# Gathered token rows turned on VectorE in 32x32 blocks instead of on TensorE, in one layer of a hybrid trunk with experts

## The reference

```python
def swiglu(x, w_gate, w_up, w_down):
    return (jax.nn.silu(x @ w_gate) * (x @ w_up)) @ w_down
...
def moe_ffn(xf, w_router, router_bias, w_eg, w_eu, w_ed, w_sg, w_su, w_sd):
    ...                                  # scores, groups, top 8 of 64, weights top_w
    x_pad = jnp.concatenate([xf, jnp.zeros((1, D), xf.dtype)], axis=0)
    def expert_block(args):
        tok, e = args
        xb = x_pad[tok]
        return swiglu(xb, w_eg[e], w_eu[e], w_ed[e])
    y = lax.map(expert_block, (buf_tok.reshape(n_blocks, MOE_BLK), block_e)).reshape(P, D)
    y = y * buf_w[:, None].astype(y.dtype)
    routed = jnp.zeros((N + 1, D), y.dtype).at[buf_tok].add(y)[:N]
    return routed + swiglu(xf, w_sg, w_su, w_sd)
```

## Time and profile before

| | |
|---|---|
| median of 3 runs | 1494.25 us (1493.85 to 1494.46) |
| span of the profiled execution | 1490.5 us |
| median less that span | 3.75 us |
| TensorE busy | 1470.0 us, 99% |
| VectorE busy | 660.9 us, 44% |
| ScalarE busy | 299.4 us, 20% |
| GpSimd busy | 663.8 us, 45% |
| front, up to the first routed matmul | 526 us |

### The profile page before, as it was taken

The page is one execution under the profiler, slowest core; times in us unless marked ns, Lnnn a source line. Parts: engine busy times, 40 slices in busy tenths (PEclk is TensorE's granted clock), DMA queues, the critical chain, the costliest instruction groups (busy, mean ns, idle before and its releaser), DMA issues.

```text
span 1490.5 us, 24090 instructions
## 1 busy us (share of the span) xinstructions
PE 1470.0 (99%) x6687; PEld 652.1 (44%) x6688; DVE 660.9 (44%) x892; ACT 299.4 (20%) x568; POOL 663.8 (45%) x626
## 2 busy tenths in 40 slices
PE   7999999999999999999999999999999999999998
PEld 3556556556565433333333333333333333333333
DVE  2344444454355454444444444444444444444432
ACT  1223323323323201111111111111111111111110
POOL 3010222212302525566655666655666556665541
PEclk9999999999999999999999999999999999999999
DMA  9511201202155579999998988888899898998938
GB/s 346 192 56 37 78 29 50 79 8 71 52 219 202 177 280 283 304 292 295 300 356 253 320 285 259 256 254 252 262 351 348 275 321 265 300 300 250 329 58 213
DMA packets 74637, 330.06 MB, mean 221 GB/s; under 512 B 14647, under 2 KB 16184, under 8 KB 48932
## 3 DMA queue, kind: packets, MB, share of 16 engines
q1 hardware_dynamic: 45140, 249.62, 45.1%
q0 software_dynamic: 29456, 79.93, 22.7%
HBM read 282.74 MB, written 65.11 MB: 233 GB/s over the span
## 4 chain that ended last, share of the span: by engine, by line
PE 94%; DMA 3%; DVE 1%; issue 1%; ACT 0%; SPq 0%; DVEq 0%; POOL 0%; POOLq 0%; ACTq 0%
PE psP L733 55%; PE psW L733 30%; PE psT L892 5%; DMA area<-x_dram 1%; DMA wts<-in_w_in_dram 1%; PE psW L955 1%; PE psW L784 1%; PE psT L826 0%; PE psT L810 0%; PE psT L741 0%; DMA out_dram<-area,sidx 0%; PE psW L761 0%; DMA x_dram<-area,sidx 0%; DVE area L1423 0%; DVE st_s L1433 0%
## 5 line engine op out<-in xcount | busy, mean ns | idle before, releaser
L733 PE MATMUL psP<-wts,bias 128*64 (+1 forms) x1296 | 574.0, 595 | 1.2 <-issue 1.1
L733 PE MATMUL psP<-area,bias 128*64 128x512 f32 x1264 | 559.4, 595 | 0.0
L733 PE MATMUL psW<-wts,area 128*64 (+2 forms) x1592 | 426.2, 592 | 0.7 <-ACT area L1305 0.5
L733 PEld LDWEIGHTS psP<-wts,bias 128*64 128x64 f32 (+1 forms) x1296 | 172.4, 138 | 336.4 <-issue 336.4
L689 POOL DMA_INDIRECT out_dram<-area,sidx x79 | 173.0, 2190 | 286.9 <-ACT area L1250 215.5
L733 PE MATMUL psP<-wts,area 128*128 128x512 f32 (+1 forms) x704 | 287.8, 560 | 6.2 <-DMA wts<-in_w_in_dram 4.8
L733 PEld LDWEIGHTS psW<-wts,area 128*64 128x64 f32 (+1 forms) x1592 | 150.1, 147 | 249.3 <-issue 247.7
L689 POOL DMA_INDIRECT x_dram<-area,sidx x79 | 247.0, 3127 | 26.6 <-issue 24.0
L1656 DVE COPY wts<-wts 128x2048 f32 x79 | 97.0, 1228 | 298.6 <-issue 298.6
L1648 DVE COPY area<-wts 128x4096 f32 x79 | 181.5, 2297 | 25.2 <-issue 20.7
L733 PEld LDWEIGHTS psP<-wts,area 128*128 128x128 f32 x704 | 131.1, 191 | 136.3 <-issue 126.5
(11 more groups left out here) (224 smaller groups left out, 870.3 us busy)
## 6 DMA issues: line engine op xcount, KB each, us to landing
wts<-in_w_exp_gate_dram SPq DMA_DIRECT2D x64, 1024.0 KB, 8.9
wts<-in_w_exp_up_dram SPq DMA_DIRECT2D x64, 1024.0 KB, 12.2
wts<-in_w_exp_down_dram SPq DMA_DIRECT2D x64, 1024.0 KB, 7.0
wts<-in_w_in_dram SPq DMA_DIRECT2D x4, 2048.0 KB, 18.0
area<-in_x_dram SPq DMA_DIRECT2D x8, 512.0 KB, 4.1
wts<-in_w_out_dram SPq DMA_DIRECT2D x1, 4096.0 KB, 18.4
area<-u_dram SPq DMA_DIRECT2D x16, 256.0 KB, 2.9
xn_dram<-area POOLq DMA_DIRECT2D x8, 512.0 KB, 3.0
```

The source lines that it names most:

```text
L733: return nc.tensor.matmul(out_, lhsT, rhs, start=start, stop=stop)
```

## The change

TensorE's `t_job` and VectorE's `read_xT` go. A new VectorE function `turn_x` reads the gathered rows from SBUF and writes `xT[par]` by sixteen transposing operations. One operation takes 32 tokens (a quarter of the partitions of `xg`) and, of each of the eight 128-column blocks, 32 columns; it turns eight 32x32 blocks and writes them to a quarter of the partitions of `xT[par]`. All bytes end where they were before. `turn_x` waits for the gather itself; the gathers wait for `s_xT_ready` instead of `s_xg_t`, with the same counts. In the loop `turn_x` stands where `read_xT` stood; in the written-out start `copy_dn(0)` and `copy_dn(1)` now stand ahead of the turn. Both weight copies stay on VectorE.

```diff
--- before.py
+++ after.py
@@ -53,6 +53,7 @@
     FT = FE // P
     assert NT == 8 and KT == 8 and NKV == 2 and DC == DA == 512 and FT == 2
     HB = P // 2
+    QUAD = 32
     JMAX = S * TOPK // P + NE // 2
     JT = JMAX + 6
     MIN_JOBS = S * TOPK // P
@@ -277,7 +278,6 @@
         s_tab_t = sem("tab_t")
         s_tab = sem("tab")
         s_sc_tab = sem("sc_tab")
-        s_xg_t = sem("xg_t")
         s_gu = sem("gu")
         s_silu = sem("silu")
         s_h_ready = sem("h_ready")
@@ -659,7 +659,7 @@
 
             def gather(j, par, copies):
 
-                pool.wait_ge(s_xg_t, j - (NSH + 1))
+                pool.wait_ge(s_xT_ready, j - (NSH + 1))
                 nc.gpsimd.tensor_copy(gidx[:, par:par + 1], tab_i[:, bass.ds(j - NSH, 1)]).then_inc(s_idx_cp, 1)
                 pool.wait_ge(s_idx_cp, copies + 1)
                 carry(pool)
@@ -669,7 +669,7 @@
 
             def first_gather(r):
                 if r >= 2:
-                    pool.wait_ge(s_xg_t, r - 1)
+                    pool.wait_ge(s_xT_ready, r - 1)
                 pool.indirect_dma_start(out=xg[:, r % 2], out_offset=None, in_=xn_dram[:, :],
                                         in_offset=bass.IndirectOffsetOnAxis(ap=tab_i[:, r:r + 1], axis=0),
                                         bounds_check=S - 1, oob_is_err=False).then_inc(g_ld[r % 2], 16)
@@ -883,15 +883,6 @@
                     t_x(NN)
                 out_project(T, 1)
 
-            def t_job(j, par, nth):
-
-                pe.wait_ge(g_ld[par], nth * 16)
-                if not (isinstance(j, int) and j == NSH):
-                    pe.wait_ge(s_xT_ready, j - NSH)
-                for k in range(KT):
-                    i = nc.tensor.transpose(psT[:, k, :], xg[:, par, k * P:(k + 1) * P], ident[:, :])
-                i.then_inc(s_xg_t, 1)
-
             def gate_up_late(t, ks):
                 buf, ld = shared_place(NSH + t)
                 if 0 in ks:
@@ -1053,8 +1044,6 @@
             down(2)
             t_h(4, psP[:, side(4), :])
             down(3)
-            t_job(NSH, 0, 1)
-            t_job(NSH + 1, 1, 1)
 
             def jobs(i, ks):
                 for k in ks:
@@ -1063,7 +1052,6 @@
                     now = pe.value_load(ring_i[0:1, bass.ds(r + 1, 1)], min_val=1, max_val=NE)
                     gate_up_halves(r + NSH, k, (now % NSLOT) * SLOTW)
                     down_halves(r + NSH - 1, (was % NSLOT) * SLOTW)
-                    t_job(r + NSH + 2, k, i + 2)
                     t_h(r + NSH, psW[:, 0, :])
 
             one = routed_jobs(pe, 1, jobs, counts)
@@ -1607,10 +1595,15 @@
             conv_gate(tiles[0])
             y_conv_rms(tiles[0])
 
-            def read_xT(j, par):
-                dve.wait_ge(s_xg_t, j - (NSH - 1))
+            def turn_x(j, par, nth):
+                dve.wait_ge(g_ld[par], nth * 16)
                 dve.wait_ge(s_gu, j - 1)
-                V.tensor_copy(xT[par], psT[:, :, :]).then_inc(s_xT_ready, 1)
+                for a in range(P // QUAD):
+                    rows = xg[a * QUAD:(a + 1) * QUAD, par, :].rearrange("t (k p) -> t k p", k=KT)
+                    for q in range(P // QUAD):
+                        i = V.transpose(xT[par][q * QUAD:(q + 1) * QUAD, :, a * QUAD:(a + 1) * QUAD],
+                                        rows[:, :, q * QUAD:(q + 1) * QUAD])
+                i.then_inc(s_xT_ready, 1)
 
             def h_mul(j, par, w):
 
@@ -1742,19 +1735,19 @@
             dve.wait_ge(s_gu, 3)
             dve.wait_ge(s_xnT_st, 16 * NT)
             copy_gu(0, 0)
-            read_xT(NSH, 0)
+            turn_x(NSH, 0, 1)
             read_shared(3, side(3))
-            read_xT(NSH + 1, 1)
+            turn_x(NSH + 1, 1, 1)
             dve.wait_ge(s_xn_st, 16 * NT)
             copy_gu(1, 1)
             h_mul(NSH, 0, tab_w[:, 0:1])
             read_shared(NSH - 1, side(NSH - 1))
-            read_xT(NSH + 2, 0)
             copy_dn(0)
+            turn_x(NSH + 2, 0, 2)
             copy_gu(2, 0)
             h_mul(NSH + 1, 1, tab_w[:, 1:2])
-            read_xT(NSH + 3, 1)
             copy_dn(1)
+            turn_x(NSH + 3, 1, 2)
             copy_gu(3, 1)
 
             def jobs(i, ks):
@@ -1762,7 +1755,7 @@
                     r = i * 2 + (2 + k)
                     h_mul(r + NSH, k, tab_w[:, bass.ds(r, 1)])
                     copy_dn(r)
-                    read_xT(r + (NSH + 2), k)
+                    turn_x(r + (NSH + 2), k, i + 3)
                     copy_gu(r + 2, k)
 
             one = routed_jobs(dve, 2, jobs)
```

## The result

| | before | changed kernel |
|---|---|---|
| median of the runs | 1494.05 us (4 runs, 1491.36 to 1494.46) | 1657.56 us (4 runs, 1655.84 to 1658.61) |
| span of the profiled execution | 1490.5 us | 1656.7 us |
| mean granted clock of TensorE over the span | 1.000 | 0.953 |
| mean routed job, `t_h` to `t_h`, from the fourth on | 11.67 us | 13.71 us |

The changed kernel takes 1.110 times as long, with an interval of 1.1085 to 1.1116. The forecast was 1459 us, with a range up to 1512; 1657.56 is 198.6 above the forecast.

A forecast was written before the change was run, and what follows sets the result against it. TensorE was taken as the bound; with its wait for VectorE in every second job, two jobs take 22.41 us, 11.20 each (before 11.69). 74 x 0.485 = 35.9, net 35 us, gives 1459 us; range 1440 to 1512.

The forecast's parts named there:

- The bound, and TensorE's part: TensorE, 99% busy, bounds the kernel; without the transposes its own work falls 0.82 to 10.87 us a job.
- TensorE stays the bound all through: Rival: transposes at 0.31 or less, or a shorter 1.80, give 60 us gain, 1434 us; chance 0.07.
- 1.80: On VectorE, copy_dn starts 1.80 us after the end of the down projection down(r-1).
- The price of a transpose: In VectorE's turn, 0.35 us for each 32x256 transposing operation, sixteen of them 5.60; range 0.335 to 0.42.
- 22.41: Loop over two jobs through VectorE and TensorE: 11.54 + 0.42 + 6.92 + 3.53 us, 11.20 a job.
- the rival of 1525: VectorE becomes the bound, transposes costing more than 0.41 each; at 0.46, 12.08 us a job; chance 0.17.
- `t_h` to gate/up, 0.42: On TensorE, the step from t_h to the first gate/up pair, taken as 0.42 us in the two-job loop.
- the forecast's 0.67: TensorE's t_h waits 0.67 us for VectorE's h_mul, in every second job.
- The start: First routed gate/up starts at 528.7, not 526.47, 2.2 us late; the fourth job starts 0.9 late.
- VectorE's queue: Register work of copy_gu, 2.5 us, hides if the queue takes several transposes ahead; cost taken as nothing.
- The rival of 1515: VectorE's queue takes only two ahead, so copy_gu starts later: 1.5 us more in two jobs; chance 0.08.
- GpSimd's slip, the weights, the transfers: Gather slips 1.2 us and weights get longer, both at no cost; rival that transfers bind, 1474, chance 0.08.

The follow-up runs named there:

- dn_act: Changed kernel with all sixteen transposes, but copy_dn moved from VectorE to ScalarE behind read_h; 1438.08 us, ratio 0.9627.
- the probe: Changed kernel with the turn replaced by fifteen operations of six kinds, transposing and plain, on 32 and 128 partitions, to time them; 1593.89 us.
- twelve_of_16: Changed kernel with twelve of the sixteen transposing operations, a quarter of the turned rows left out; 1529.65 us, ratio 1.0235.
- twelve_loads_early: Changed kernel with twelve of the sixteen transposes and TensorE's register loads for the next job ahead of t_h; 1477.83 us, ratio 0.9892.
- pe_loads_early: Changed kernel with all sixteen transposes and TensorE's register loads for the next job ahead of t_h, not behind it; 1568.51 us, ratio 1.0491.

## Why the prediction was wrong, point by point

**The bound, and TensorE's part: right.** Its own job without L892 is 10.82 us in dn_act (forecast 10.87). The prediction's rival "TensorE stays the bound all through", at 1434, is near what dn_act gives (1438), but by another edit, not by cheaper transposes or a shorter 1.80; for the change as it was made it was wrong.

**The price of a transpose: a term too small.** 0.35 was taken, 0.449 was measured (7.17 for sixteen in the timeline, 7.34 with the gap up to `copy_gu`). The row that it was taken from has 128 partitions, and the step "partitions work side by side, so 32 of them cost what 128 do" is the one that failed. In the probe it holds for the length of one operation (0.44 and 0.45) and not for the start of the next (0.44 and 0.37). The other row of the same group, 0.46 for operations that wait for each other, was nearer. By that step alone the loop is 22.41 + 1.74 = 24.15 us, 12.08 a job, which is the rival of 1525 (0.17, with all that is slower at 0.25); the measured time is 133 us above that too, and no case of the prediction reached it. A slip beside it: with 0.375 each the prediction's own sum gives 1474, not the 1470 at the end of its range; nothing hangs on it.

**`t_h` to gate/up, 0.42: a step that turns the sign by itself.** The prediction moved 0.42 over from the earlier trace rows, where eight transposes of 0.82 us stood ahead of `t_h` and `h_mul` was done 2.9 us before it (kernel before, 909.18 to 912.04):

```profile
908.50 0.68 DVE L1620 SCALAR_TENSOR_TENSOR dsq<-dsq,area,psP 128x256 f32<-128x256 f32 x1 [2.39 <-ACT dsq L1230]
...
912.04 0.38 PE L955 MATMUL psW<-ident,dsq 128*128 128x128 f32 x2
```

TensorE's first register load for the next job ran at 909.2, when `h_mul` had ended, under the last matmuls of the down projection. The row of the kernel before shows it, and the prediction had not read it:

```profile
L1062 PEldq TENSOR_LOAD <-ring_i x1: 305/305/305, 909.2 to 909.2; - x1
```

The prediction asked whether VectorE's register work stays hidden and did not ask that of TensorE. A wait put into a queue also stops the register work behind it, here 1.87 us at the end of a lap and 1.5 inside it, in every second job, 1.7 x 38 = 64 us in all. twelve_of_16 has the forecast's turn and is slower than the kernel before; twelve_loads_early takes this one thing away, and comes to 11.30 a job against the forecast's 11.20. Neither this step nor the price was the only one: each alone would have made the kernel slower (twelve_of_16 by 36 us, pe_loads_early by 75).

**The clock: left out.** Gate/up was costed at 6.92 at full clock. Behind a stand of 4.5 us it took 8.41, 3.4 of it at the 1.2 GHz level. The 1.49 us come in every second job, 55 us over the jobs. With a wait near the forecast's 0.67 it mostly doesn't come: twelve_of_16 stands still for 1.9 to 2.6 us in such a job and keeps 6.91 in 34 of 38. So this term is a consequence of the other two together.

**The start: too small.** 2.2 us late were forecast for the first gate/up, 3.7 measured (530.16 against 526.47), by the longer turn. TensorE had stood still for 8.87 us then and ran at the low clock for the next 4.8, which the forecast didn't have, and gate/up and the later turns were longer as in the loop. By the fourth job it was 13.0 instead of 0.9. TensorE's row and the window behind it, in the changed kernel:

```profile
530.16 1.11 PE L733 MATMUL psP<-wts,bias 128*64 x1 [8.87 <-DVE bias L1604]
```

```profile
530.00:534.80 4.80, 4.64 (x12) 0.52 0.61 183
```

**VectorE's queue: the result right, the number not.** The forecast needed the queue to take several transposes ahead. In the changed kernel the register work of `copy_gu` starts with the twelfth of sixteen, so four are still ahead of it in the queue; VectorE's timeline from there, and its queue:

```profile
1018.38 0.89 DVE L1604 STREAM_TRANSPOSE bias<-area 32x256 f32<-32x256 f32 x2
```

```profile
L1639 DVEq TENSOR_LOAD <-ringB_i x1: 315/315/315, 1018.9 to 1018.9; - x1
```

These four and the twelfth, at 0.449 each, cover the register work down to the gap of 0.17. It was so in 78 of the 79 turns; behind the first one stands no such register work. The Trainium skill, "Advanced Engine Details and Errata", Engine Queue Depths, gives 8 for VectorE; these rows show 4, and the rows decide. The rival of 1515 (two ahead) was wrong.

**GpSimd's slip, the weights, the transfers: right.** GpSimd now waits 236.4 us for the turn before it copies the index, in 75 jobs, and that costs nothing in turn: the scatter still waits for ScalarE (166.3 us), ScalarE waits for scatters 62.7 us where it was 68.4 before, and VectorE started no turn late for lack of rows. `copy_gu` waits for issue 19.8 of its 20.7 idle us. The DMA share is 0.80 to 0.81 over the jobs of the changed kernel, and 0.93 and 0.89 in dn_act's two windows, where a job takes 10.82.

## What to carry to other kernels

Before you cost a wait at its own length, look at what is queued behind the waiting instruction, on that same engine: register loads and branches start only when it is let go, and the producer must be done earlier by their length (here 1.7 to 2.4 us) than the consumer gets there. When work moves to an engine that has idle time, look where in its order the idle time lies. Here VectorE had 54% of it, but in front of a copy that waits for TensorE; the work that was put behind that copy cost 163 us, and the same work gained 55 once the copy was out of the way. And don't price a row of operations on 32 partitions by the distance of operations on 128.

## What the runs showed of the hardware that was not expected

- On VectorE operations of 32 partitions x 256 elements, float32, each on other input or output partitions than the last, follow each other at their whole length: 0.44 to 0.45 us transposing, 0.30 plain. On 128 partitions transposing operations overlap: 256 elements 0.45 long, next after 0.37.
- TensorE's register instructions behind a matmul whose semaphore is not there yet stand still even while earlier matmuls run: in dn_act the branch (L360) ran at 1010.5, when `h_mul` ended at 1010.42, with the down projection running until 1012.5.
- After a stretch of 4.5 us with 0.44 us of matmuls the granted clock was at the 1.2 GHz level for 3.4 us, nearly each time; after 1.9 to 2.6 us it mostly stayed at 2.4 (twelve_of_16: 6 low stretches in the whole span, the changed kernel 41).
- A copy of 2048 float32 elements takes 1.91 us on ScalarE and 1.23 on VectorE. ScalarE had the room for it: it was 20% busy in the kernel before.
